# Gates before or after the branch products: swapping the order of two products in the mixing stage

## The reference, cut to what matters

```python
def token_mixing(x, w_in, ..., w_branch, w_o, lam_init, cos, sin):
    z = x @ w_in
    a_b, a_c, a_v, ..., n_g, m_g = jnp.split(z, SPLIT_POINTS, axis=-1)
    y_a = a_b * causal_dwconv(a_c * a_v, conv_a_w)
    ...
    gates = jax.nn.sigmoid(m_g).reshape(b, s, N_BRANCHES, D_MODEL)
    merged = (gates[:, :, 0] * (y_a @ w_branch[0])
              + gates[:, :, 1] * (y_b @ w_branch[1])
              + gates[:, :, 2] * (y_c @ w_branch[2]))
    return merged @ w_o
```

## Time and profile before

| | |
|---|---|
| median of 3 runs | 4064.23 us (4056.22 to 4065.22) |
| the profiled execution | 4064.23 us |
| its span | 4062.4 us, mean granted TensorE clock 0.954 |
| PE busy | 3704.1 us (91% of the span), 19754 matmuls |
| DVE busy | 2076.4 us (51%) |
| ACT busy | 1453.4 us (36%) |
| POOL busy | 599.9 us (15%) |
| branch stage of layer 0 | about 340 to 627 us of the span |
| branch stage of layer 1 | about 1448 to 1734 us |

### The profile page before, as it was taken

How to read it: one execution, slowest core, us unless ns; L and a number is a source line. 1 busy time by engine, 2 the same in 40 slices (tenths; PEclk the granted TensorE clock), 3 DMA queues, 4 the chain that set the end, 5 groups by cost and what they waited for, 6 DMA issues and landing times.

```text
span 4062.4 us, 50599 instructions
## 1 busy us (share of the span) xinstructions
PE 3704.1 (91%) x19754; PEld 2969.4 (73%) x19754; DVE 2076.4 (51%) x3698; ACT 1453.4 (36%) x2259; POOL 599.9 (15%) x665
## 2 busy tenths in 40 slices
PE   8889997999888899989997887899999789898998
PEld 6666676787666666768885856688888579777777
DVE  4646664664456466556653635445364352554332
ACT  3445633442224356334423345221211233543221
POOL 1111122011220011221011100024252022000000
PEclk9989999999989899989998988999999889999999
DMA  4111132323231112332233100023231111111222
GB/s 151 59 63 68 63 134 83 130 104 129 89 115 64 52 63 73 137 108 104 109 125 123 53 1 11 32 88 113 83 121 71 54 53 61 60 58 66 100 88 78
DMA packets 65999, 339.07 MB, mean 83 GB/s; under 512 B 6752, under 2 KB 8288, under 8 KB 40160
## 3 DMA queue, kind: packets, MB, share of 16 engines
q1 hardware_dynamic: 65760, 335.84, 22.7%
HBM read 327.43 MB, written 8.39 MB: 83 GB/s over the span
## 4 chain that ended last, share of the span: by engine, by line
PE 76%; DVE 12%; ACT 8%; issue 2%; POOL 2%; DMA 0%; DVEq 0%; ACTq 0%; POOLq 0%; SPq 0%
PE ps L1615 23%; PE ps L1617 22%; PE ps L1616 22%; ACT wh L1747 2%; DVE wl L1855 2%; PE ps L1604 2%; PE ps L1728 2%; PE ps L1624 2%; PE ps L1709 1%; DVE tt L1863 1%; POOL xt L2099 1%; PE ps L1721 1%; DVE pb L2076 1%; DVE acc L1863 1%; DVE hl L1863 1%
## 5 line engine op out<-in xcount | busy, mean ns | idle before, releaser
L1747 ACT ACTIVATE wh<-raw 128x2048 fp32r<-128x2048 f32 (+2 forms) x277 | 457.8, 1653 | 942.1 <-PE ps L1617 938.1
L1855 DVE TENSOR_TENSOR wl<-raw,wh 128x2048 fp32r<-128x2048 f32 (+2 forms) x277 | 551.0, 1989 | 395.7 <-ACT wh L1747 374.1
L1615 PE MATMUL ps<-hh,wh 128*128 128x512 f32 (+1 forms) x1248 | 449.5, 360 | 33.0 <-DVE hl L1863 33.0
L2099 POOL TENSOR_TENSOR lt<-lt,cs 128x1024 f32<-128x1024 f32 x96 | 184.1, 1917 | 1790.0 <-DVE acc L1863 1790.0
L1616 PE MATMUL ps<-hl,wh 128*128 128x512 f32 (+1 forms) x1248 | 444.9, 357 | 0.0
L1617 PE MATMUL ps<-hh,wl 128*128 128x512 f32 (+1 forms) x1248 | 444.8, 356 | 0.0
L1615 PE MATMUL ps<-xhb,wh 128*128 128x512 f32 x832 | 371.1, 446 | 13.6 <-DVE xlb L1855 10.9
L1617 PE MATMUL ps<-xhb,wl 128*128 128x512 f32 x832 | 338.8, 407 | 0.0
L1616 PE MATMUL ps<-xlb,wh 128*128 128x512 f32 x832 | 337.9, 406 | 0.0
L1615 PE MATMUL ps<-xha,wh 128*128 128x512 f32 x704 | 283.5, 403 | 29.0 <-DVE wl L1855 26.5
L1615 PEld LDWEIGHTS ps<-hh,wh 128*128 128x128 f32 x1248 | 236.9, 190 | 73.2 <-DVE hl L1863 36.1
(11 more groups left out here) (258 smaller groups left out, 7276.4 us busy)
## 6 DMA issues: line engine op xcount, KB each, us to landing
raw<-in_wts SPq DMA_DIRECT2D x199, 1024.0 KB, 4.8
lt<-in_wts SPq DMA_DIRECT2D x110, 512.0 KB, 3.5
raw<-in_wts SPq DMA_DIRECT2D x44, 512.0 KB, 3.5
raw<-in_wts SPq DMA_DIRECT2D x32, 448.0 KB, 3.1
x_scratch<-xt SPq DMA_DIRECT2D x3, 2048.0 KB, 9.1
xt<-x_scratch SPq DMA_DIRECT2D x3, 2048.0 KB, 8.1
oe<-in_relb SPq DMA_DIRECT2D x16, 384.0 KB, 3.5
bt<-in_big SPq DMA_DIRECT2D x1, 2688.0 KB, 12.8
```

The lines of the kernel that those rows point to most:

```text
L1615: T.matmul(u.out, u.sh, u.mh, start=u.first, stop=False)
L1747: A.activation(u.h, u.raw, ACT.Copy).then_inc(*act.inc())
L1855: V.tensor_tensor(o_, a, b, op).then_inc(*dve.inc())
L2099: G.tensor_tensor(o_, a, b, op).then_inc(*pool.inc())
```

## The change

The two products of a step change places: `wb` comes first, in the list of panels and in `branch`. Its two chunks are copied out of PSUM by ACT into `GS[0]` and `GS[1]`, then the `mg` panel follows, and both its sigmoids go to the one buffer `GG`. `gate` then reads two SBUF tiles and waits for the sigmoid alone. In branches 1 and 2 the first `wb` panel uses the order by k over both chunks (`both_chunks` with `first`), where a y row is needed only when its k comes. `yt`, the token that lets the next split of y start, is now the last matmul of `wb`; the calls of `split` still stand after `branch` returns.

```diff
@@ panel_plan
+                add((("wb", br, mp), l), 1024, wbr)
                 c0 = 4376 + br * D + mp * 256
                 win(l, ("mg", br, mp), np.arange(c0, c0 + 256))
-                add((("wb", br, mp), l), 1024, wbr)
                 add_ada()
@@ mix
-            gs_free = [gs_free[0], ab_free[1]]
+            gs_free = [[y_ks[-1]], [y_ks[-1]], [y_ks[-1]]]
...
                 for mp in range(4):
-                    pg, s_ = get((("mg", br, mp), l), 8), []
-                    for m in range(2):
-                        r, t = fm_chunk(pg, m, 8, XH, XL, TOK, GR, xw)
-                        s_.append(evac(GS[m], r[0].ap, [t], ACT.Sigmoid, free=gs_free[m]))
-                        r[0].free = [s_[m]]
-                    pg.done(t)
                     pb_ = get((("wb", br, mp), l), 4)
+                    for m, r in enumerate(both_chunks(pb_, 4, YH, YL, TOK, GR, y_ks, mp == 0 and br > 0)):
+                        r[0].free = [evac(GS[m], r[0].ap, [r[0].w], free=gs_free[m])]
+                    yt = r[0].w
+                    pg = get((("mg", br, mp), l), 8)
                     for m in range(2):
-                        r, t = fm_chunk(pb_, m, 4, YH, YL, TOK, GR, [], y_ks)
+                        r, t = fm_chunk(pg, m, 8, XH, XL, TOK, GR, xw)
+                        s_ = evac(GG, r[0].ap, [r[0].w], ACT.Sigmoid, free=gs_free[2])
+                        if m == 1:
+                            pg.done(t)
+                        r[0].free = [s_]
                         mo = MG[:, 2 * mp + m, :]
-                        u = add("gate", first=br == 0, m=mo, g=GS[m], y=r[0].ap, came=[s_[m], t])
-                        r[0].free = gs_free[m] = [DVE(u)]
+                        u = add("gate", first=br == 0, m=mo, g=GG, y=GS[m], came=s_)
+                        gs_free[m] = gs_free[2] = [DVE(u)]
                         if br == 2:
                             m_ks.append(split(mo, MH[:, 2 * mp + m, :], ML[:, 2 * mp + m, :], [DVE(u)], [mw]))
-                    pb_.done(t)
-                return t
+                return yt
@@ dve_program
                 elif kind == "gate":
-                    for t in u.came:
-                        dve.wait_ge(*at(t))
+                    dve.wait_ge(*at(u.came))
```

More of the change, by code:

```diff
@@ L1041, in branch @@
                 for mp in range(4):
-                    pg, s_ = get((("mg", br, mp), l), 8), []
+                    pb_ = get((("wb", br, mp), l), 4)
+                    for m, r in enumerate(both_chunks(pb_, 4, YH, YL, TOK, GR, y_ks, mp == 0 and br > 0)):
+                        r[0].free = [evac(GS[m], r[0].ap, [r[0].w], free=gs_free[m])]
+                    yt = r[0].w
+                    pg = get((("mg", br, mp), l), 8)
                     for m in range(2):
                         r, t = fm_chunk(pg, m, 8, XH, XL, TOK, GR, xw)
-                        s_.append(evac(GS[m], r[0].ap, [t], ACT.Sigmoid, free=gs_free[m]))
-                        r[0].free = [s_[m]]
-                    pg.done(t)
-                    pb_ = get((("wb", br, mp), l), 4)
-                    for m in range(2):
-                        r, t = fm_chunk(pb_, m, 4, YH, YL, TOK, GR, [], y_ks)
+                        s_ = evac(GG, r[0].ap, [r[0].w], ACT.Sigmoid, free=gs_free[2])
+                        if m == 1:
+                            pg.done(t)
+                        r[0].free = [s_]
                         mo = MG[:, 2 * mp + m, :]
-                        u = add("gate", first=br == 0, m=mo, g=GS[m], y=r[0].ap, came=[s_[m], t])
-                        r[0].free = gs_free[m] = [DVE(u)]
+                        u = add("gate", first=br == 0, m=mo, g=GG, y=GS[m], came=s_)
+                        gs_free[m] = gs_free[2] = [DVE(u)]
                         if br == 2:
                             m_ks.append(split(mo, MH[:, 2 * mp + m, :], ML[:, 2 * mp + m, :], [DVE(u)], [mw]))
-                    pb_.done(t)
-                return t
+                return yt
             yt = branch(0, y_ks)
```

## The result

| | before | after |
|---|---|---|
| median of 4 runs each | 4064.72 us (4056.22 to 4067.36) | 4126.28 us (4122.95 to 4128.82) |
| span of the profiled run | 4062.4 us | 4125.3 us |
| mean granted TensorE clock | 0.954 | 0.949 |

The ratio is 1.0154, 95% interval 1.0137 to 1.0172: slower by 61.6 us. The forecast was 4091 us with a range of 4070 to 4108. The direction was right, the size was not, and the time lies outside the range.

A forecast was written before the change was run, and what follows sets the result against it. PE was taken to bound the kernel, busy 91% of the span. Added waits and slow clock of 22.4 us per layer, 44.8, less 18.0 removed, gave +26.8 on 4064.2: 4091 us, range 4070 to 4108.

The forecast's parts named there:

- The signs that I had named for a right forecast: yl waits of 2.7, 5.4, 4.1 us per layer, slow clock behind the last two; wl near 0.6; end 1 us, layer 0.
- (a): Start of branch 0: PE waits 2.7 us for the fourth row of y; no slow clock counted.
- (b): Boundary of branches 0 and 1: y splits queue behind the last sigmoid and panel split; wait 5.4 us, slow clock 1.7.
- the first rival: No measurable change: the same waits at their lower ends, no slow clock; 4070.6 us at worst; chance 0.10.
- (c): Boundary of branches 1 and 2: PE waits 4.1 us for the y splits, plus 1.7 us of slow clock.
- (d): Steps of branch 2: wl comes late behind the second gate and ml; 0.6 us three times, 1.8 per layer.
- (e): Steps inside the attention part: PE waits for score banks behind late wl and acc rows; 5.0 us per layer, replacing 1.77.
- (f): Stage end: sigmoid frees the bank w_o wants; layer 0 waits 1.0 us instead of 4.1, 4.8 won; layer 1 wins 1.1.
- (g): 48 more copies on ACT, 28.8 us, priced at nothing except in the attention steps; uncovered, up to 28.8.
- the faster one: Rival: ACT-freed banks remove all earlier waits and y splits slip under the gate panel; 4044 us, chance 0.05.
- The slower one: Rival: copies delay ptb copies and panel splits, half of them, 14.4 us, on PE's path; 4109 us, chance 0.13.

The follow-up runs named there:

- e8: Changed kernel with the ada panel between wb and mg and the next y's splits ahead of the last mg panel: 4066.62 us, ratio 1.0007.
- e1: Changed kernel, but during the branches ada_sum takes its PSUM bank from the attention's ring of two: 4113.93 us, ratio 1.0120.
- e2: Changed kernel with the ada panel listed between wb and mg instead of behind mg: 4085.35 us, ratio 1.0053.
- e7: Kernel before with only the ada panel moved, to between mg and wb instead of behind wb: 4173.89 us, ratio 1.0278.
- e5: Kernel before, mg first, with only ACT's 48 copies of wb chunks into SBUF and gate reading SBUF: 4063.96 us, ratio 0.9999.
- e10: Changed kernel with a second tile for the second sigmoid of each step, nothing else: 4128.1 us, ratio 1.0169.
- e3: Changed kernel with the next branch's y splits recorded behind the last wb product, ahead of its mg panel: 4098.39 us, ratio 1.0083.
- e4: Changed kernel with only the first step of branch 0 in the old order and with the old gate: 4120.91 us, ratio 1.0146.

## Why the prediction was wrong

By its own steps, layer 0 and layer 1 alike unless said. The signs that I had named for a right forecast nearly all came (2.66, 5.53 and 3.97 us, `wl` at 0.38, the end at 0.78), and the time was wrong all the same, because the list of signs held only the waits that I had thought of.

- (a) start: forecast 2.7 us, measured 2.66. The open question was the dip; there is one, 1.7 us per layer, not counted.
- (b) first boundary: 5.4 us and a dip, measured 5.53 us and twice a dip's loss. The chain on ACT and DVE ran as worked out. (In the first rival the same chain without the exponentials should be 4.1 less the attention product, 3.2 us, and not 3.6; that rival would start 0.8 us lower.)
- (c) second boundary: 4.1 us and a dip, measured 3.97 and one dip (0.72 over 6 us).
- (d) 0.6 us three times, measured 0.37 to 0.39.
- **(e) the step that failed.** Forecast 5.0 us per layer as waits for score banks, measured 17.5 us in six waits for the bank of `wb` chunk 0, and four dips behind them. I followed the chain on ACT and DVE to the scores and asked who needs the scores' banks. I had the ring of three in my list and the copies in step (g) "at nothing, except as in (e)", but never counted which bank each chunk gets once `ada_sum` changes sides. The waits for score banks that I priced do not occur at all in the changed kernel, since PE has already been held at the bank; a wait for them (2.50 us) comes up in e8, where the others are gone. e1 shows the bank as the cause with the copies as late as they were; e2 and e7 show from both sides that the panel's place decides. That it is not ACT's load, e5 shows; that it is not the shared tile, e10.
- (f) end: 1.0 us, measured 0.78, and none in layer 1.
- (g) copies at nothing: held for their load on ACT (e5, in the old order). "Except as in (e)" was the opening: PE never waits for `ptb` in these stages, but for six of the copies themselves.
- Not in the sum: 3.6 us won ahead of layer 0's stage, because the panel split there is the 1024 one. In layer 1 it is 7.5 us: 1.9 us of idle PE, and a clock of 0.96 instead of 0.89 over the last 80 us ahead of the stage.

In numbers: (e) was short by 12.5 us per layer, the dips by six per layer (eight against two), 10.2 us, the steps (a) to (d) and (f) were together 0.9 and 0.7 us too high, and the gains ahead of the stages, 3.6 and 7.5, were left out. That makes 18.2 us for layer 0 and 14.5 for layer 1, 32.7 in all; the landmarks miss the forecasts of the layers (12.4 and 14.4) by 16.6 and 16.2, 32.8 in all. With the 3.3 us of the second block it is the miss of 4126.3 - 4091 = 35.3 us to within a microsecond. The range failed for the same reason: its upper end was the copies' uncovered share, and even (e) doubled, 10 us more, ends at 4101; no side of it had dips behind (e).

Of the rivals, the faster one fell as reasoned: ACT's list does have the splits behind the last sigmoid. Moving them (e3) won 28 us of the loss, and with the panel moved too (e8) the kernel is only back to even. The slower one had the right direction and ended 17 us too low, by a mechanism that did not happen: no `ptb` copy was delayed onto PE's path.

## What to carry to other kernels

When work is reordered around a ring of banks, write out the sequence of banks chunk by chunk, with every occasional user in its place, and for each hand-over how many products lie between the last use and the next. Then ask of each hand-over how late the reader of that bank is. A user that comes once per step can turn a ring of three into one of two for some products, and its place decides which of them wait; a move of it by one panel cost 113 us here, more than the whole reorder. Price each wait together with the slow clock behind it: in layer 0 of this kernel that was half as much again (11.9 us on 22.0).

## What the runs showed of the hardware

The loss of granted clock at a wait of PE was not even with the wait's length. In the changed kernel, waits of 1.67 us and less left it at 1.00. Waits of 2.66 to 4.1 us went with 0.72 over 6 us (part of it at 1.2 GHz), 1.7 us lost, and the 5.53 us wait with 0.58 over 8 us, 3.4 us lost. The other traces show that the length alone does not decide. The 2.71 us wait of e4 left the clock at 1.00 (379 to 385), and so did the 2.50 us wait of e8 (444 to 450), while a 1.86 us wait in e8 went with 0.72 over 6 us (562 to 568), and the 3.92 us wait of e2 with 0.58 over 8 us (566 to 574). So a count of dips from waits is an estimate that can be off by a dip at each.

An ACT instruction behind a table load started 0.01 us after it at the places shown, and under 0.03 us after it behind 47 of the 74 table loads in the trace of the kernel before.
